# Halved row transposes, an input chunk split before the last down chunk, and cross attention in steps of two heads

## What is computed

```
for l in range(DEPTH_2):
    h = rmsnorm(x, norm_mix[l])
    (a_q, ..., g_br) = jnp.split(h @ w_in[l], offsets, axis=-1)
    o_a = swa_mixer(...); o_b = nsa_mixer(...); o_c = mla_mixer(...)
    merged = (g[:, :, 0] * (o_a @ w_br_a[l])
              + g[:, :, 1] * (o_b @ w_br_b[l])
              + g[:, :, 2] * (o_c @ w_br_c[l]))
    x = x + merged @ w_out[l]
    x = x + cross_attn(rmsnorm(x, norm_xattn[l]), rmsnorm(mem, norm_mem[l]),
                       w_xq[l], w_xkv[l], w_xo[l])
    h = rmsnorm(x, norm_ffn[l])
    gate_h, up_h = jnp.split(h @ w_gate_up[l], 2, axis=-1)
    x = x + (jax.nn.silu(gate_h) * up_h) @ w_down[l]
```

## Time and profile before

| what | value |
|---|---|
| time, median of 3 runs | 1960.24 us (1958.13 to 1961.72) |
| time of the profiled execution | 1956.37 us |
| its span, first to last instruction | 1954.4 us |
| mean granted TensorE clock | 0.942 |
| PE busy | 1748.7 us, 89% of the span |
| chain that ended last | PE 66%, issue 12%, DVE 9%, DMA 8%, ACT 4% |

### The profile page before, as it was taken

One profiled execution on the slowest core, in us unless ns is written; L12 is line 12 of the kernel. 1 busy time (PEld: TensorE's weight loads), 2 busy tenths in 40 slices (PEclk: granted clock), 3 DMA queues, 4 the chain that ended last, 5 costly groups with the idle time before them and its releaser, 6 DMA issues.

```text
span 1954.4 us, 21694 instructions
## 1 busy us (share of the span) xinstructions
PE 1748.7 (89%) x9183; PEld 1277.1 (65%) x9183; DVE 851.2 (44%) x1205; ACT 597.3 (31%) x879; POOL 26.7 (1%) x80
## 2 busy tenths in 40 slices
PE   5999999988999969999988679998899988859997
PEld 1897555444434337565677679987656667659996
DVE  4675153252101145353465336544543365534543
ACT  1453210000111124243534334334333543433441
POOL 1000010000000000000000000000000000000000
PEclk9899898988999979999999889999999998979999
DMA  7455222657999944413234136453433233414542
GB/s 243 172 190 197 88 86 86 247 194 291 396 393 395 393 162 164 148 52 129 107 116 168 62 105 199 174 194 130 147 108 109 96 138 118 165 43 160 186 176 93
DMA packets 181579, 333.23 MB, mean 171 GB/s; under 512 B 17523, under 2 KB 68981, under 8 KB 181493
## 3 DMA queue, kind: packets, MB, share of 16 engines
q1 hardware_dynamic: 175680, 325.89, 47.0%
q10 hardware_dynamic: 5814, 6.11, 0.9%
HBM read 330.94 MB, written 1.05 MB: 170 GB/s over the span
## 4 chain that ended last, share of the span: by engine, by line
PE 66%; issue 12%; DVE 9%; DMA 8%; ACT 4%; POOL 0%; SPq 0%; POOLq 0%; DVEq 0%; ACTq 0%
PE ps_g L624 18%; PE ps_g L639 12%; PE ps_g L1040 7%; DMA arena<-in_w_up_dram 5%; PE ps_g L924 4%; PE ps_o L694 3%; DVE ring_r L1762 2%; PE ps_p L624 2%; PE ps_s L624 2%; DMA ring<-in_w_mod_dram 2%; PE ps_s L665 2%; PE ps_x L599 1%; PE ps_p L684 1%; PE ps_g L726 1%; PE ps_p L1175 1%
## 5 line engine op out<-in xcount | busy, mean ns | idle before, releaser
L1762 DVE TENSOR_TENSOR ring_r<-ring,late_w 128x4096 fp32r<-128x4096 f32 (+1 forms) x52 | 225.8, 4342 | 162.6 <-ACT late_w L1416 162.6
L1416 ACT ACTIVATE late_w<-ring 128x4096 fp32r<-128x4096 f32 (+1 forms) x52 | 185.0, 3557 | 240.4 <-PE ps_g L639 112.1
L639 PE MATMUL ps_g<-h_t_r,late_w 128*128 128x256 f32 x768 | 217.9, 284 | 0.0
L639 PE MATMUL ps_g<-hf_high,late_w 128*128 128x256 f32 x704 | 199.3, 283 | 3.8 <-DVE h_t_r L1750 3.8
L639 PE MATMUL ps_g<-hf_high,ring_r 128*128 128x256 f32 x704 | 198.8, 282 | 0.0
L1040 PE MATMUL ps_g<-ring,h_t 128*128 128x512 f32 x320 | 147.4, 606 | 0.0
L639 PEld LDWEIGHTS ps_g<-h_t_r,late_w 128*128 128x128 f32 x768 | 147.3, 192 | 0.0
L639 PEld LDWEIGHTS ps_g<-hf_high,late_w 128*128 128x128 f32 x704 | 133.8, 190 | 4.5 <-DVE h_t_r L1750 4.5
L639 PEld LDWEIGHTS ps_g<-hf_high,ring_r 128*128 128x128 f32 x704 | 135.0, 192 | 0.0
L924 PE MATMUL ps_g<-ring,arena 128*64 128x512 f32 x384 | 118.7, 611 | 13.3 <-DMA arena<-in_w_up_dram 11.6
L1040 PEld LDWEIGHTS ps_g<-ring,h_t 128*128 128x128 f32 x320 | 58.8, 191 | 65.0 <-issue 63.8
(11 more groups left out here) (569 smaller groups left out, 3367.0 us busy)
## 6 DMA issues: line engine op xcount, KB each, us to landing
ring<-in_w_in_dram SPq DMA_DIRECT2D x31, 2048.0 KB, 7.7
ring<-in_w_gate_up_dram SPq DMA_DIRECT2D x44, 1024.0 KB, 7.0
ring<-in_w_gate_dram SPq DMA_DIRECT2D x16, 2048.0 KB, 17.3
arena<-in_w_down_dram SPq DMA_DIRECT2D x16, 2048.0 KB, 15.7
ring<-in_w_mod_dram SPq DMA_DIRECT2D x12, 2048.0 KB, 9.6
ring<-in_w_down_dram SPq DMA_DIRECT2D x10, 2048.0 KB, 8.2
ring<-in_w_up_dram SPq DMA_DIRECT2D x8, 2048.0 KB, 18.2
arena<-in_w_up_dram SPq DMA_DIRECT2D x8, 2048.0 KB, 19.9
```

The costliest lines, as they stand in the source:

```text
L639: ins = pe.matmul(b.ap[:, (f % 2) * SEQ:(f % 2 + 1) * SEQ], a[:, k, f * P:(f + 1) * P], x[:, k, :], start=k == 0 and i == 0, stop=k == nk ...
L1416: act.activation(high_of(name, rnd)[:, 0:n], ring[:, slot, 0:n], ACT.Copy).then_inc(high_ready.sem, 1)
L1762: dve.tensor_tensor(ring_r[:, slot, 0:n], ring[:, slot, 0:n], high_of(name, rnd)[:, 0:n].bitcast(F32), ALU.subtract).then_inc(low_ready.se ...
```

## The change

It has these parts.

1. `turn_rows` can do the second half alone. The second half of the `mem` transposes stands between the two halves of `brc`; the first half of `mg` stands in the middle of `memk`, its second half behind it; the first half of `hx` stands between the two row blocks of `memv` and the second in the middle of its second block. PE waits for the second half's low parts only in the middle of a following product. DVE and ACT make low and high parts in halves accordingly, and `hx_high` gets a place of its own.
2. DVE and ACT make the parts of `ox` ahead of those of `gu0`, and the parts of `hf` ahead of those of `gu1`.
3. Cross attention runs in four steps of two heads.
4. High and low part of the next layer's `in0` are made ahead of those of `fd5`. In layer 1 PE, ACT and DVE take `in4` ahead of `in3`; SP's order of loads stays.
5. At the start of each layer DVE makes `mix_scale` ahead of the first low part that follows, where it stood behind.

```
-IN_ORDERS = ([1, 0, 2, 3, 4, 5], [0, 1, 2, 3, 4, 5])
+IN_ORDERS = ([1, 0, 2, 3, 4, 5], [0, 1, 2, 4, 3, 5])
...
-X_STEPS = [("x", 0, qb) for qb in range(TB)]
+X_STEPS = [("x", pp, qb) for pp in range(2) for qb in range(TB)]
...
-        hx_high, mem_low, h_low = mem_high, view_r("mem_low", S_AT, KD, SEQ), h_t_r
+        hx_high, mem_low, h_low = view_r("hx_high", 2 * PW, KD, SEQ), view_r("mem_low", S_AT, KD, SEQ), h_t_r
...
+                pe.wait_ge(rows.sem, rows.at("layer", "mem", l))
+                mem_half(0)
+                turned("layer", "oc", 2, l)
+                w = split_chunk("brc", KF, D, l)
+                product_rows("layer", "brc", "brc0", (o_high["c"], o_low["c"]), w, KF, 0, HALF, l, last=False)
+                mem_half(1)
+                product_rows("layer", "brc", "brc1", (o_high["c"], o_low["c"]), w, KF, HALF, HALF, l)
+                turned("layer", "mem", 4, l)
...
+                product_turned("layer", "memk", "memk", (mem_high, mem_low), split_chunk("memk", KD, HALF, l), KD, l, second_half=merged_ready)
+                merged_half(1)
+                turned("layer", "mg", 2, l, 0)
+                product_rows("layer", "out0", "out0", (mg_high, h_low), split_chunk("out0", KD, HALF, l), KD, 0, HALF, l,
+                             midway=lambda: turned("layer", "mg", 4, l))
...
+                query_half(0)
+                product_rows("layer", "memv", "memv", (mem_high, mem_low), w, KD, 0, HALF, l, blocks=[1], midway=lambda: query_half(1))
+                turned("layer", "hx", 2, l, 0)
+                product_turned("layer", "xq", "xq", (hx_high, h_low), split_chunk("xq", KD, HALF, l), KD, l, midway=lambda: turned("layer", "hx", 4, l))
...
-                make_low("in1" if l else "in0", rnd=l)
                 dve.wait_ge(rstd_ready.sem, rstd_ready.at("layer", "mix", l))
                 dve.tensor_scalar(mix_scale[:, 1, :], mix_scale[:, 0, :], 0.5, None, ALU.mult).then_inc(mix_half, 1)
+                make_low("in1" if l else "in0", rnd=l)
...
-                make_low("gu0", rnd=l)
                 turned_low("ox", KF, o_low["x"], o_high["x"], l)
+                make_low("gu0", rnd=l)
...
                 for c in range(2, 6):
+                    if c == 5 and l + 1 < LAYERS:
+                        make_low("in0", rnd=l + 1)
                     make_low(f"fd{c}", rnd=l)
```

More of the change, by code:

```diff
@@ L582, in end, with turned, turn_rows @@
                     b.end(rounds)
[L584 to L586 removed]
+            def turned(part, tag, n, rnd=0, first=None):
+                for r in range(max(0, n - 2) if first is None else first, n):
                     b = (X, O)[r % 2]
                     pe.wait_ge(b.free, b.nth(part, f"{tag}{r}", rnd))
[L590 to L592 removed]
+            def turn_rows(tag, pieces, rnd=0, size=P, ready={}, first=0):
+                for r in range(2 * first, len(pieces), 2):
                     if r // 2 in ready:
@@ L1140, in _ @@
-                product_turned("layer", "memk", "memk", (mem_high, mem_low), split_chunk("memk", KD, HALF, l), KD, l)
-                pe.wait_ge(rows.sem, rows.at("layer", "merged", l))
-                turn_rows("mg", [lambda tb, k=k: merged[:, tb, k * P:(k + 1) * P] for k in range(KD)], l)
-                turned("layer", "mg", 4, l)
-                for name in ["out0", "out1"]:
-                    product_rows("layer", name, name, (mg_high, h_low), split_chunk(name, KD, HALF, l), KD, 0, HALF, l)
@@ L1148, in _, with mem_half, merged_half, query_half @@
-                product_rows("layer", "memv", "memv", (mem_high, mem_low), split_chunk("memv", KD, HALF, l), KD, 0, HALF, l)
+                def mem_half(r):
+                    turn_rows("mem", [lambda tb, k=k: mem_rows[:, tb, k * P:(k + 1) * P] for k in range(4 * r + 4)], l, first=2 * r)
+                def merged_half(r):
+                    turn_rows("mg", [lambda tb, k=k: merged[:, tb, k * P:(k + 1) * P] for k in range(4 * r + 4)], l, first=2 * r)
+                def query_half(r):
+                    turn_rows("hx", [lambda tb, k=k: h_rows[:, tb, k * P:(k + 1) * P] for k in range(4 * r + 4)], l, first=2 * r)
@@ L1149, in _ @@
+                product_rows("layer", "out0", "out0", (mg_high, h_low), split_chunk("out0", KD, HALF, l), KD, 0, HALF, l,
+                             midway=lambda: turned("layer", "mg", 4, l))
+                product_rows("layer", "out1", "out1", (mg_high, h_low), split_chunk("out1", KD, HALF, l), KD, 0, HALF, l)
+                w = split_chunk("memv", KD, HALF, l)
+                product_rows("layer", "memv", "memv", (mem_high, mem_low), w, KD, 0, HALF, l, last=False, blocks=[0])
                 pe.wait_ge(rows.sem, rows.at("layer", "xattn", l))
-                turn_rows("hx", [lambda tb, k=k: h_rows[:, tb, k * P:(k + 1) * P] for k in range(KD)], l)
@@ L1390, in copy_turned, with take @@
                     act.activation(d, b.ap[0:size, 0:d.shape[1] * SEQ].rearrange("p (k n) -> p k n", n=SEQ), ACT.Copy).then_inc(b.free, 1)
-            def take(part, name, dst, func=ACT.Copy, scale=1.0, rnd=0):
-                for i, b in enumerate(banks_of(part, name)):
+            def take(part, name, dst, func=ACT.Copy, scale=1.0, rnd=0, only=range(2)):
+                for i in only:
+                    b = banks_of(part, name)[i]
                     d = dst(i)
```

123 lines of the change are left out of this document (69 added, 54 removed).

## The result

| | before | after |
|---|---|---|
| median, same chip, 4 runs each | 1960.98 us | 1901.62 us (1897.49 to 1907.57) |
| ratio, 95% interval | | 0.9694 [0.9671, 0.9716] |
| profiled execution, span | 1956.4, 1954.4 us | 1897.49, 1895.4 us |
| granted clock, mean | 0.942 | 0.955 |

What follows compares the result with a forecast made beforehand. PE bounds the kernel, by standing still or running at its low clock. Two layers of 25.6 us (51.2), plus 1.1, less 4.4 and 1.0, give 46.9 off: 1909.5 or 1913.3 by baseline, taken as 1912, range 1903 to 1926.

Steps and rivals of the forecast that it cites:

- Mem, brc, memk, mg, out0: Each layer, mem's transposes to out1: PE's waits for low parts nearly vanish, 49.7 us becomes 37.6, 12.1 gained.
- Out1, memv, hx, xq: Each layer, out1 to the attention scores: 40.9 us becomes 37.0, with 1.6 of waits left; 3.9 gained.
- Cross attention and ox: Each layer, scores to xo: four overlapping steps and the moved low part (4.4) make 26.3 us 20.1; 6.3 gained.
- Norm and hf: Each layer, ahead of gu0: hf's third filling starts earlier, with gu1's parts behind it; 3.3 us gained.
- The sign that PE's waits for `h_rows` would come near 0.1: Listed among signs of being right: PE's waits for the normalized rows would be near 0.1.
- In0 ahead of fd5: At the mix transposes: PE's 0.80 us wait goes as in0's low part moves into idle time; 1.1 gained with what follows.
- In4 ahead of in3: Layer 1's fourth input chunk: in4 lands 5.0 us after in3 but is needed first; 4.4 us lost.
- The rival that it costs nothing: Layer 1's in4: PE's start is not set by the load's landing, so 4.4 us stay, 1908; chance 0.08.
- Mix_scale first: Layer 0's in0: DVE first waits for POOL's root and makes mix_scale, delaying in0's low part; 1.0 us lost.
- The clock did not fall at the inserted transposes: Rival at mem, mg and hx: each inserted place costs 1.6 us by a clock fall, 19 in all, 1931; chance 0.09.
- no gain was lost to a lower grant: Rival, whole kernel: closer packed products make the chip grant less, so it gets slower, 1994 at 0.90; chance 0.02.
- That four steps give nothing: Rival in cross attention: only the moved low part's 4.4 us or 2 less is gained, 1916 to 1920; chance 0.13.

Runs made afterwards that it cites:

- e3: The changed kernel with gu0's high and low parts ahead of those of ox again; 1914.53 us, ratio to the kernel before 0.9748.
- e4: The kernel before with only two order swaps: parts of ox ahead of gu0's, parts of hf ahead of gu1's; 1940.95 us, ratio 0.9895.
- e2: The changed kernel with SP also issuing in4's load ahead of in3's in layer 1; 1890.23 us, ratio to the kernel before 0.9637.
- e5: The changed kernel with cross attention in two steps of four heads again; 1916.88 us, ratio to the kernel before 0.9772.
- e7: e2 with 11 unused 128 by 256 matmuls in PE's idle stretch over the norm ahead of hf; 1888.84 us, ratio to the kernel before 0.9620.
- e8: e2 with 48 filler transposes of 128 by 128 in PE's idle stretch over the norm; 1891.95 us, ratio to the kernel before 0.9644.
- e1: The changed kernel with in3 taken ahead of in4 again in layer 1; 1897.86 us, ratio to the kernel before 0.9667.
- e11: e9 with in0's low part ahead of mix_scale again in layer 0; 1885.50 us, ratio to the kernel before 0.9629.
- e9: e2 with filler matmuls at xo (3), over the norm (11), ahead of hf's third filling (2) and gu0 (3); 1886.59 us, ratio 0.9632.

## Why the prediction was right in kind and short in size

- **Mem, brc, memk, mg, out0.** Right: 12.2 and 12.7 against 12.1. The walk's waits (none at `brc`, 0.5 at `memk`) came as none and 0.21.
- **Out1, memv, hx, xq.** Right: 4.2 against 3.9. PE waits 1.00 in all, at `xq`, where the walk had 1.6, and `xq`'s 96 matmuls take 11.5, measured as the prediction did (1058.12 to 0.73 before 1070.39), at the lower end of what was said.
- **Cross attention and ox.** The step that failed, in two places. Its walk ended at `xo`'s start: 7.0 and 7.2 against 6.3 (its own numbers, 26.3 less 20.1, give 6.2), where I had added 0.4 for outputs at the low clock, and they ran at full clock. Its split, 4.4 for the moved low part and the rest for the steps, holds only if the steps come first (4.7 by e3); with two steps the low part gives 3.6 (e4). Before the change `gu0`'s op began at 1109.37 and ACT had the first high part of `ox` at 1110.15, so 0.8 of its 4.42 us would have passed in any case. And `xo` itself had no term. The prediction said that "a gap costs more than itself" and showed `xo`'s start at 0.50, but it priced only the gap's length. With 1.62 instead of 5.15 ahead of it `xo` took 10.95 instead of 13.44 and 13.58: 5.1 more in the two layers. e3 and e4 tie this to the gap, but a gap of 1.62 does not always keep the clock: e2 had the fall in one layer, e5, e7 and e8 in each. Even then `xo` took 12.3 to 12.6, against 12.95 to 13.58 behind the long gaps of the kernel before and e3. So 5.1 is what this execution gained, luck included; over the sixteen layers with that gap and no filler (nine near 10.97, seven near 12.5) the mean is 11.6, and the term for two layers 3.8.
- **Norm and hf.** Right: 3.4 against 3.3. The 1.89 ahead of `gu0` stayed. The sign that PE's waits for `h_rows` would come near 0.1 failed: they are 5.49 in each layer, as before. It belonged to no term, since the sum kept this wait, so it moves none of the numbers.
- **In0 ahead of fd5.** 0.74 against 1.1: the wait of 0.80 is gone, the next one grew from 3.69 to 3.96.
- **In4 ahead of in3.** The gap grew by 4.39 against 4.4. In the changed kernel the stretch grew by 3.5 only, since the input products ahead of it had 0.9 less of low clock; e1 puts the edit at 3.8. The rival that it costs nothing is refuted.
- **Mix_scale first.** 0.85, and 0.9 in e11 against e9, against 1.0. Freed POOL and ACT gave nothing back. The Trainium skill, "SBUF — State Buffer" (the part on the shared port pair), says that such ops of DVE and GpSimd lock each other out; the root's 4.79 and 0.69 us agree with it, and it moved no time on PE.
- **The rivals.** The clock did not fall at the inserted transposes, and no gain was lost to a lower grant (0.955 against 0.942). That four steps give nothing is refuted by e5.
- **The sum.** The profiled execution is 12.0 below 1909.5. The first five rows of the table give 8.2 of it (5.1 at `xo`, 1.6 in attention, 0.8 in the first, 0.6 in the second, 0.1 in the last). The rest is luck of this execution: the part ahead of the second block started layer 0's mix transposes 2.0 earlier, the branch product `bra` of layer 0 took 11.2 instead of 12.2, and the 0.9 at the input products. The median is 4.1 above the profiled execution, so of the 10.4 by which it misses 1912, 8.2 is the mis-sized part if the other executions had `xo` as this one did, and 6.9 with `xo`'s mean of 11.6; what is left is within what the medians scatter.

What stays open: why the clock falls in one layer and not in the next behind the same instructions, and how much the chip has to do with it. No run was made that steers it without filling the gap, and none that repeats one kernel on several chips.

## What to carry to other kernels

When an edit shortens a wait of PE from some 5 us to some 1.5, price the product behind it at both clocks, as its own term; the forecast was right wherever it walked the waits and short where it stopped at the start of a product. A chunk that is moved ahead in the order of use must be moved in the queue that loads it, too: here the first alone cost 3.8 us and both together gained 6. And where waits can't be removed, spare matmuls in a free bank held the clock over them at `gu0`, but the gain of some 3 us per layer disappears in the scatter of the whole unless it is read by stretches.

## What the runs showed of the hardware

- Behind the same instructions and the same gap of 1.62 us the granted clock was 0.50 in one layer and 1.00 in the other of one execution. Gaps of 5.15 and 6.31 us had 0.50 behind them in all four layers seen; with the gap filled to 0.32 it was 1.00 in all six, which ran on another chip.
- 48 fp32 transposes in an idle stretch (5.40 us) held the grant at 1.00 (e8), as 11 matmuls of 128 by 256 did (4.91 us, e7).
- POOL's root of 128 by 2 took 4.79 us while DVE made a weight's low part, and 0.69 with DVE waiting, in e11 and e9, which differ in this order alone.
- Code that is alike in all kernels ended between 720 and 731 us in thirteen profiled executions.
